# A decoder layer on one core: uneven chunks of rows without the first index queries, and state updates, last builds and pages in another order

## What is computed

```python
h = jnp.einsum('btd,de->bte', rms_norm(x, ln_g), w_in)
a_q, a_k, a_v, a_gate, i_q, i_w, i_k, h_q, h_f, h_i, h_gate = split_columns(h)
...
s = jnp.einsum('bthd,bsd->bths', iq.astype(F32), ik.astype(F32)) * IDX_DIM ** -0.5
score = jnp.einsum('bths,bth->bts', jax.nn.relu(s), iw)
...
_, idx = lax.top_k(score, topk)       # topk = 256, causal
```

## Time and profile before

| | us |
|---|---|
| median of 3 runs | 805.73 |
| lowest and highest run | 801.14, 806.96 |
| the profiled execution | 804.48 |
| its span | 802.8 |
| TensorE busy | 760.7 |
| VectorE busy | 542.8 |
| ScalarE busy | 420.7 |
| GpSimd busy | 396.2 |

### The profile page before, as it was taken

How to read it: one execution, slowest core, us unless ns; L and a number is a source line. 1 busy time by engine, 2 the same in 40 slices (tenths; PEclk the granted TensorE clock), 3 DMA queues, 4 the chain that set the end, 5 groups by cost and what they waited for, 6 DMA issues and landing times.

```text
span 802.8 us, 20221 instructions
## 1 busy us (share of the span) xinstructions
PE 760.7 (95%) x7576; PEld 704.1 (88%) x7576; DVE 542.8 (68%) x1110; ACT 420.7 (52%) x1274; POOL 396.2 (49%) x576
## 2 busy tenths in 40 slices
PE   3999999999999999999989999979799998999998
PEld 3889989899999999999988999868588878898998
DVE  3644767998999999879994846678446367555121
ACT  6765775346365686577554746554435554422110
POOL 3454735437735693579396435249932427510220
PEclk9999999999999999999999999999999999999999
DMA  8303021221102312231202345594644634341632
GB/s 282 93 21 86 14 90 41 66 66 42 53 3 80 94 47 74 80 95 47 74 28 75 124 127 166 161 253 134 155 153 140 206 122 142 124 139 55 229 101 82
DMA packets 69927, 83.57 MB, mean 104 GB/s; under 512 B 20458, under 2 KB 55962, under 8 KB 69578
## 3 DMA queue, kind: packets, MB, share of 16 engines
q1 hardware_dynamic: 65146, 68.68, 27.3%
q0 software_dynamic: 4688, 13.64, 6.1%
HBM read 64.95 MB, written 17.34 MB: 103 GB/s over the span
## 4 chain that ended last, share of the span: by engine, by line
PE 76%; POOL 8%; DVE 5%; issue 4%; ACT 4%; DMA 2%; POOLq 0%; SPq 0%; ACTq 0%; DVEq 0%
PE psum L2298 25%; PE psum L2295 16%; PE psum L1331 11%; PE psum L2214 3%; PE psum L1264 3%; PE psum L1280 3%; POOL w_low L549 2%; PE psum L2172 2%; PE psum L2191 1%; PE psum L1242 1%; PE psum L1238 1%; PE psum L2150 1%; PE psum L1244 1%; DMA page_keys<-in_cache_kt 1%; POOL page_keys L613 1%
## 5 line engine op out<-in xcount | busy, mean ns | idle before, releaser
L2298 PE MATMUL psum<-w_high,xT_high 128*128 128x256 f32 x640 | 183.2, 286 | 0.3 <-ACT stage L1804 0.3
L2298 PE MATMUL psum<-w_low,xT_high 128*128 128x256 f32 x640 | 179.8, 281 | 0.0
L2298 PE MATMUL psum<-w_high,xT_low 128*128 128x256 f32 x640 | 179.6, 281 | 0.0
L549 POOL TENSOR_TENSOR w_low<-w_raw,w_high 128x256 fp32r<-128x256 f32 (+1 forms) x144 | 105.5, 769 | 65.0 <-ACT w_high L1686 54.7
L2298 PEld LDWEIGHTS psum<-w_high,xT_high 128*128 128x128 f32 x640 | 120.4, 188 | 2.4 <-ACT stage L1804 0.5
L2298 PEld LDWEIGHTS psum<-w_high,xT_low 128*128 128x128 f32 x640 | 120.5, 188 | 0.4
L2298 PEld LDWEIGHTS psum<-w_low,xT_high 128*128 128x128 f32 x640 | 120.6, 188 | 0.0
L2295 PE MATMUL psum<-xT_high,w_high 128*128 128x384 f32 (+3 forms) x312 | 103.8, 333 | 0.9 <-POOL w_low L549 0.9
L2295 PE MATMUL psum<-xT_high,w_low 128*128 128x384 f32 (+3 forms) x312 | 100.3, 322 | 0.0
L2295 PE MATMUL psum<-xT_low,w_high 128*128 128x384 f32 (+3 forms) x312 | 100.3, 322 | 0.0
L2037 DVE TENSOR_SCALAR_CACHE_REDUCE flag_count<-scores,candidate 128x512 f16<-128x512 f32 (+2 forms) x96 | 96.9, 1009 | 0.0
(11 more groups left out here) (334 smaller groups left out, 1857.3 us busy)
## 6 DMA issues: line engine op xcount, KB each, us to landing
w_raw<-in_w_main SPq DMA_DIRECT2D x40, 512.0 KB, 4.0
x_rows<-in_x_prompt SPq DMA_DIRECT2D x8, 512.0 KB, 6.2
page_keys<-in_cache_kt SPq DMA_DIRECT2D x32, 128.0 KB, 3.9
page_keys<-in_cache_kt POOLq DMA_DIRECT2D x32, 128.0 KB, 5.7
page_values<-in_cache_v SPq DMA_DIRECT2D x32, 128.0 KB, 3.5
page_values<-in_cache_v POOLq DMA_DIRECT2D x32, 128.0 KB, 3.9
x_res<-in_x_prompt SPq DMA_DIRECT2D x32, 128.0 KB
out<-y_rows SPq DMA_DIRECT2D x32, 128.0 KB
```

Of the source, the lines that this page charges most:

```text
L549: last = gp.tensor_tensor(WL[:, u % 2, 4 * h + k, 0:w], raw(u)[:, h, k, 0:w], f(WH[:, u % 2, 4 * h + k, 0:w]), ALU.subtract)
L2298: last = pe.matmul(ps(BANK[n], w, rows(i)), x[:, k, row0(i):row0(i) + rows(i)], ww[:, sl, k, 0:w], start=first, stop=final)
```

## The change

It has four parts.

1. **Chunks.** The rows of x are cut in 256, 384 and 392 instead of 384, 384 and 264. The first chunk's index queries are not computed (queries under 256 keep all keys): unit 0 has 7 jobs instead of 9, unit 2 five instead of seven, and all later job numbers fall by 4. With them `X_AT`, `GROUPS` and the numbers of the sample's index products move: these now come after jobs 20 and 21, which is behind the first and second job of unit 4; the last item is in job 18, the second to last of unit 3. The index loads go in another order: 9 in a rotation of three blocks, the splits' constants, the split of unit 2, three of the fourth block, 20 in a rotation of four, and only then the split of unit 3. GpSimd does not wait for scaled rows before its first split.
2. **State updates.** In unit 13, GpSimd splits only the first half of unit 14's weights, in two quarters, and VectorE splits the other half before its last mask.
3. **Last builds.** The builds are in the order of tiles 1 to 7, 0, at other jobs. The last build's queries have bank 5 and are finished by VectorE after the first maximum of the tail. The first scores take the upper 512 keys first and wait for the last build's keys only for the lower ones. The low part of the bias moves one build later, the samples' rows two builds later.
4. **Pages.** GpSimd issues one of its last three sets of pages before the padded query tile and the other two before the state output.

```diff
-CHUNKS = [(0, 384), (384, 384), (768, 264)]
+TILES = [1, 2, 3, 4, 5, 6, 7, 0]
+CHUNKS = [(0, 256), (256, 384), (640, 392)]
+CHUNK_ROWS = [(0, 1), (2, 3, 4), (5, 6, 7, 8)]
+ROWS_BY_ACT = (1, 4, 7)
...
-FRONT = [(x, b, c) for c in range(3) for x, b in ((0, 0), (1, 0), (1, 1))]
-IX_JOBS = 7
+FRONT = [(x, b, c) for c in range(3) for x, b in ((0, 0), (1, 0), (1, 1)) if x == 0 or c > 0]
+IX_JOBS = 5
...
-X_AT = {(2, 3): (1, range(4)), (2, 7): (1, range(4, 8)), (4, 7): (2, range(4)), (5, 3): (2, range(4, 8))}
+X_AT = {(0, 7): (1, range(8)), (3, 3): (2, range(4)), (3, 7): (2, range(4, 8))}
...
-        out = [(u, "T", b, c) for c in range(3) for b in range(2)]
+        out = [(u, "T", b, c) for c in (1, 2) for b in range(2)]
...
-GROUPS = {8: [0], 9: [1], 10: [2], 11: [3], 12: [4], 13: [5, 6], 15: [7], 16: [8], 17: [9], 18: [10], 19: [11]}
+GROUPS = {6: [0], 7: [1], 8: [2], 9: [3, 4], 11: [5], 12: [6], 13: [7], 14: [8], 15: [9], 16: [10], 17: [11]}
...
-KEYS_ROWS_AT, SAMPLE_AT, SAMPLE_SUM_AT = 7, 22, 23
+KEYS_ROWS_AT, SAMPLE_AT, SAMPLE_SUM_AT = 5, 20, 21
...
-BUILD_AT = {JOB0[LAST] + q: i for q, i in ((4, 0), (6, 1), (8, 2), (10, 3), (12, 4), (14, 5), (15, 6), (16, 7))}
+BUILD_Q = (4, 5, 7, 8, 10, 12, 14, 16)
+BUILD_AT = {JOB0[LAST] + q: b for b, q in enumerate(BUILD_Q)}
+LOAD_Q = {BUILD_Q[b] + 1: b + 2 for b in range(NT - 2)}
+STORE_Q = {3: 0, 4: 1, 7: 2, 8: 3, 10: 4, 11: 5, 14: 6}
...
+        def quarter_at(u, q):
+            return ({1: 0, 4: 1} if u == HGU[-1] else {1: 0, 2: 1, 3: 2, 4: 3}).get(q)
...
                 last.then_inc(s["sample_state_ready"], 1)
+                load_key_pages(gp, numbers, 11)
                 gp.wait_ge(s["sample_state_ready"], 1)
...
             sample_state()
+            for n in (13, 15):
+                load_key_pages(gp, numbers, n)
             for hh in range(2):
...
-            for n in (11, 13, 15):
-                load_key_pages(gp, numbers, n)
...
+        def q_bank(b):
+            return 3 if b < NT - 1 else 5
...
             for i in range(NT):
-                dve_build(dve, i)
-                if i == NT - 3:
+                dve_build_keys(dve, i)
+                if i < NT - 1:
+                    dve_build_queries(dve, i)
+                if i == NT - 2:
...
-                if i == 2:
+                if i == 4:
                     dve_norm_sample(dve, link)
...
+                    if m == 0:
+                        dve_build_queries(dve, NT - 1)
...
+                    pe.wait_ge(s["q_built"], NT - 1)
+                if m == 1:
                     pe.wait_ge(s["k_built"], NT)
-                    pe.wait_ge(s["q_built"], NT)
...
-                for c0 in range(0, w, 512):
+                for c0 in (512, 0) if m == 0 else range(0, w, 512):
                     n = min(512, w - c0)
+                    if m == 0:
+                        pe.wait_ge(s["k_built"], NT - (c0 > 0))
...
-            gp.wait_ge(s["x_rows_scaled"], 2)
             split_w(gp, 0)
             split_w(gp, 1)
...
-            load_index_keys(0, 0, NPG)
+            load_index_keys(0, 3, range(3))
...
-            load_index_keys(1, 0, 3)
...
             split_w(gp, 2)
-            load_index_keys(1, 3, NPG)
-            load_index_keys(2, 0, 3)
+            gp.wait_ge(s["x_transposed"], 3 * KC)
+            load_index_keys(0, 3, (3,))
+            load_index_keys(3, NPG, range(4))
             split_w(gp, 3)
-            load_index_keys(2, 3, NPG)
-            load_index_keys(3, 0, NPG)
...
+                    if k == 5:
+                        dve.wait_ge(s["weights_low_ready"], 2 * (HGU[-1] + 1) + 1)
+                        split_half(dve, HGU[-1] + 1, 1)
                     dve_mask(dve, link, k, P, sc, w, JK, CU, MSK[:, SC0[k + 2]:SC0[k + 2] + w])
```

More of the change, by code:

```diff
@@ L1438, in load_x @@
             def load_x(g):
-                for i in range(3 * g, 3 * g + 3):
+                for i in CHUNK_ROWS[g]:
                     sp.dma_start(x_buf(i)[0:rows(i)], x_rows(i)).then_inc(s[f"x_in{i}"], 16)
@@ L1861, in _ @@
                     if n == 1:
-                        for i in (6, 7):
+                        for i in range(5, NT + 1):
                             squares(i)
-                        scale_rows(5)
-                    if n == 2:
-                        squares(NT)
+                    if n == IX_JOBS - 1:
+                        high_w(2)
                     if (n, 3) in X_AT:
@@ L2078, in _ @@
             x_roots(1)
-            for i in (3, 4):
+            for i in (2, 3):
                 scale_rows(i)
@@ L2085, in _ @@
                         low_x(*X_AT[n, 3])
+                    if n == 1:
+                        x_roots(2)
+                        for x in (5, 6, NT):
+                            scale_rows(x)
                     if n < LOWS:
@@ L2147, in transpose_x @@
                         pe.wait_ge(s["x_low_ready"], KC * c + k - 3 if c > 0 else 1)
-                    for i in range(3 * c, 3 * c + 3):
+                    for i in CHUNK_ROWS[c]:
                         r = rows(i)
```

138 lines of the change are left out of this document (69 added, 69 removed).

## The result

The changed kernel takes 813.72 us (median of 4 runs, 811.78 to 814.55) beside 804.91 for the kernel before in the same comparison: ratio 1.0111 (95% interval 1.0073 to 1.0148), slower by 1.1%. A second measurement on another occasion (`r_after`, two runs) gave 814.53 and 1.0140 (1.0087 to 1.0193). The forecast was 797 with a range of 785 to 807. The profiled execution took 814.55 us with a span of 812.5.

What follows compares the result with a forecast made beforehand. TensorE, busy 95% of the span, was taken as the bound. Terms 4 + 5.4 - 9.3 - 7 + 4.5 + 4.5 + 5.2 = +7.3 us, taken from 804.5, gave 797 us, range 785 to 807.

Steps and rivals of the forecast that it cites:

- Front: Until unit 2 starts: earlier start 2.7, fewer columns 5.4, waits gone 0.9, new stop -5; sum +4 us (1 to 7).
- Units 2 and 3: New stop at unit 3: its split, behind 23 index loads on GpSimd, 7.6 late; with restart -9.3 us (0 to -26).
- My slower rival, C: Loads held while VectorE scores, unit 3's split late by 24.4 instead of 7.6: 814 us; chance 0.08.
- Unit 4: New stop before unit 4, whose split follows the causal selections after the last item: 5.2 plus restart 1.8, -7 us.
- Updates, builds, pages: TensorE's waits for state updates, last builds and past key pages mostly go: +4.5, +4.5 and +5.2 us.
- rival B: The late stops only move, so half of the 14.2 us is lost: 804 us; chance 0.2.
- The chunks' columns: 512 fewer query columns for TensorE in the front and the same in unit 2: 5.4 us each.

Runs made afterwards that it cites:

- a2_split_first: The changed kernel with 6 index loads, then unit 3's split, then 17 loads in rotation: 798.27 us, 0.9942 of the kernel before.
- b3_dense: The kernel before, its chunks kept, with only the index loads in the changed kernel's order: 810.53 us, 1.0090 of the kernel before.
- h1_late_gap: The kernel before with change parts 2 to 4, and GpSimd waiting for its own last operation at four places per preparation: 793.72 us, 0.9880 of the kernel before.
- h3_split_first_gap: `a2_split_first` with GpSimd also waiting for its own last operation at four places per preparation: 795.49 us, 0.9901 of the kernel before.
- g1_paced: The changed kernel, loads in the same order and places, GpSimd waiting before each group of four until the previous group landed: 814.54 us, 1.0106 of the kernel before.
- a5_split_then_dense: The changed kernel with unit 3's split straight behind unit 2's and all 23 loads behind both: 817.45 us, 1.0193 of the kernel before.
- g2_f1_paced: `a2_split_first` with GpSimd's waits for scaled rows back, samples one item earlier, and a landing pause before each four loads: 800.09 us, 0.9933 of the kernel before.

## Why the prediction was wrong

**Front, +4 forecast, -1.5 measured.** This is the first step that failed, 5.5 us off and outside its 1 to 7. The start was to come 2.7 earlier and came 1.5 earlier. VectorE's root steps were priced from a row without GpSimd beside them, and I had costed the wait that GpSimd loses at nothing. With it gone, splits run beside the steps and the scaling (GpSimd's and VectorE's timelines of the changed kernel):

```profile
7.67 2.39 POOL L557 TENSOR_TENSOR w_low<-w_raw,w_high 128x72 fp32r<-128x72 f32 x8 [4.86 <-ACT w_high L1712]
20.30 6.43 POOL L557 TENSOR_TENSOR w_low<-w_raw,w_high 128x256 fp32r<-128x256 f32 x8 [10.24 <-ACT w_high L1712]
```

```profile
23.84 2.31 DVE L1973 TENSOR_SCALAR x_rows<-x_rows,x_stats 128x1024 f32<-128x1024 f32 x2
```

The scaling took 2.31 instead of 1.42, root steps 0.65 instead of 0.17. The second stop was 7.1, not 5, inside the bounds of 2 to 8; with the waits back it was 3.7 to 4.6. And I had charged no restart behind it, though I charged 1.8 behind the others: the granted clock was 0.50 from 26.2 to 30 and 0.93 on the mean from 26.21 to unit 2, which is 2.6 us. These three, 1.2, 2.1 and 2.6, are the miss; the columns themselves gave what they were to give, or a little more.

**Units 2 and 3.** This is the step whose mechanism failed, the term of -9.3 for one stop. I asked when the loads and the split would be done and got that nearly right: pitch 1.25 where I took 1.39, split 7.36 where I took 7, split 7.2 late where I said 7.6. I did not ask what an unbroken row of 20 loads does to the other engines. The sum had a stop of 9.3 with its restart; the stretch lost 15.0 (4.6 lost, where 10.4 of columns and items should have been gained), the late signals with the clock at 0.50 behind them. It took 47.8 us where `a2_split_first` takes 30.8. My slower rival, C, gave 814 and the result is 814, but that is luck, by another mechanism: it wanted loads held by VectorE's scores, each at 1.8 and more, and a split 24 late, and none of this is in the trace. The Trainium skill (page "SBUF — State Buffer", section "SBUF: two separate sides"), on which C leaned, says that VectorE and GpSimd can lock each other out for one instruction and that TensorE and ScalarE never wait on anyone there. The prediction took from this page of the Trainium skill that loads in the score stage would all pay; what the page says of descriptor writing is for VectorE's two-port modes alone, and in `b3_dense` 17 of the 21 loads of the unbroken run took 0.94 to 1.06 beside a scoring VectorE. No run here shows loads held by VectorE in the changed kernel's stretch; what is late in the changed kernel is between TensorE and ScalarE, which that rule does not cover, and a VectorE operation was held over some ten GpSimd instructions, not one.

**Unit 4.** Right to a tenth: 5.15 for 5.2, and 11.1 for 12.0 with the moved items.

**Units 5 to 8, forecast nothing, lost 4.2.** The step left out: GpSimd and VectorE keep their work there, but the small operation is held there until GpSimd's run ends. The kernel before has the two later long cases (3.89 and 3.10 us) and is spared the first, which nearly every other kernel has; `h1_late_gap` wins this stretch back with the first case gone. No view of the profile before would have given the sign of this term, but the two long cases were there to be read as a warning.

**Updates, builds, pages.** Measured +4.5, +2.7 and +4.5 for +4.5, +4.5 and +5.2. As expected the state waits went and the page wait kept a rest (2.1 for 1.5). The builds' term was too large by 1.8: 1.9 us on `qT_stack` stayed as a wait. `c_late` has these parts alone: 7.4 us in the medians, about half of the 14.2 forecast, as rival B said, but not because late stops moved: 4.1 us are lost to the held operation.

**The chunks' columns.** 10.8 us of columns do go, but with well placed loads (`a2_split_first`) the kernel is not faster than `c_late`, which has none of that gain (798.3 against 796.3). At the second S both stand at 158: the front's second stop (7 to 8) with the slow clock behind it, the moved items and unit 4's stop eat what the columns gave.

## What to carry to other kernels

Price a moved run of GpSimd work not only by when it ends, but also by how long it goes without a wait: here the long holds, up to 16 us of waits, all came some 10 us or more into an unbroken run, though not every such run held something (18 us in `h3_split_first_gap` did not). Where ScalarE or VectorE waits with no releaser in the record, or a tiny operation lasts microseconds, look at what GpSimd did in the last 10 us, and try one wait on its own last operation, which took 0.07 us here. And test an order of loads apart from the edit that it travels with: the useful parts of this change were worth 1%, and its order of loads cost nearly 2%.

## What the hardware did that I had not expected

- TensorE's signals to ScalarE came 2.4 to 14.3 us after the start of the matmul that gives them in the changed kernel, up to 15.6 in `r_after`, from 10 us into a run of indirect loads 1.25 apart. DMA traffic was low then (51 and 53 GB/s in the windows). The same loads paced (`g1_paced`), serial loads and runs under 10 us (`a2_split_first`) show none of these late signals. That breaking the run ends them is shown; that length alone brings them is not, since 18 us of loads in `h3_split_first_gap` brought none. By what mechanism a signal is late stays open, and so does whether the gaps without a releaser in TensorE's own small products (`a5_split_then_dense`, 8.6 us in 14 gaps; `g2_f1_paced`) are the same thing.
- With the old chunks (`b3_dense`) 28 us of the same loads delayed no TensorE signal and then one VectorE operation by some 5 us. Why the chunks make this difference stays open; it was not tried further.
- A VectorE operation on 128x6 took 7.3 to 8.8 us instead of 0.23 when it began 10.8 us into an unbroken run of GpSimd products, in thirteen of fifteen kernels, and ended with that run; in the other two it took 0.42. Waits of GpSimd on its own last operation, some 0.07 us each (207.69 to 207.76), end it.
